# An encoder trunk on one NeuronCore: what each stage loads for the next one, and who waits for the last stores

## What is computed

```python
for i in range(2):
    h = rmsnorm(x, ln_g[i])
    p = h @ (w_in_a if i == 0 else w_in_b)      # mixer inputs, q_mem (256), gate (1024)
    o_mix = mla_mixer(...) if i == 0 else sgu_mixer(...)          # both 768 wide
    o_mem = memory_attention(q_mem, mem, mem_norm_g[i], w_mem_kv[i], ...)   # 4 heads of 64
    o = concatenate([o_mix, o_mem], -1) * silu(gate)
    x = x + o @ w_out[i]
# sgu_mixer: u, v = gelu(uv); v = rmsnorm(v);
#   out = u * (w_s[g] @ v[chunk of 128 tokens, group g] + b_s)
```

## Time and profile before

| | |
|---|---|
| median of 3 runs | 3411.08 us (3408.62 to 3411.88) |
| the profiled execution | 3414.65 us, of which the span is 3412.9 us |
| TensorE busy (matmul / weight load) | 3222.1 us, 94% / 2763.4 us |
| VectorE, ScalarE, GpSimd busy | 1990.6, 1713.4, 1407.5 us |
| mean granted clock | 0.967 of full speed |
| mean DMA rate | 133 GB/s |

### The profile page before, as it was taken

How to read it: one execution, slowest core, us unless ns; L and a number is a source line. 1 busy time by engine, 2 the same in 40 slices (tenths; PEclk the granted TensorE clock), 3 DMA queues, 4 the chain that set the end, 5 groups by cost and what they waited for, 6 DMA issues and landing times. The chain is left out here.

```text
span 3412.9 us, 46378 instructions
## 1 busy us (share of the span) xinstructions
PE 3222.1 (94%) x17548; PEld 2763.4 (81%) x17548; DVE 1990.6 (58%) x2792; ACT 1713.4 (50%) x2472; POOL 1407.5 (41%) x916
## 2 busy tenths in 40 slices
PE   7979979999999999999899997997999979999899
PEld 7978857777777777777589996786888859999787
DVE  5638868888888888888553333444333334333432
ACT  4526647777777777777654443003232234544200
POOL 2238858999999999999710000000111000000000
PEclk9989979999999999999899998998999989999899
DMA  8958972323232233331142224886222243222565
GB/s 298 340 197 317 346 263 59 69 65 70 64 59 52 49 66 69 66 69 26 59 186 92 106 90 144 229 228 212 95 95 97 85 148 139 91 93 81 172 191 155
DMA packets 380334, 454.87 MB, mean 133 GB/s; under 512 B 51800, under 2 KB 317400, under 8 KB 367824
## 3 DMA queue, kind: packets, MB, share of 16 engines
q1 hardware_dynamic: 380112, 451.91, 42.8%
HBM read 262.07 MB, written 189.64 MB: 132 GB/s over the span
## 5 line engine op out<-in xcount | busy, mean ns | idle before, releaser
L1331 POOL TENSOR_TENSOR at_acc<-at_acc,at_ph 128x1024 f32<-128x1024 f32 x288 | 691.4, 2401 | 64.4 <-ACT at_ph L1255 48.9
L1376 DVE TENSOR_TENSOR at_pl<-at_sc,at_ph 128x1024 fp32r<-128x1024 f32 x408 | 499.0, 1223 | 127.0 <-ACT at_sc L1256 122.7
L1255 ACT ACTIVATE at_ph<-at_sc 128x1024 fp32r<-128x1024 f32 x408 | 418.5, 1026 | 291.9 <-PE at_sc L1175 283.4
L1364 DVE TENSOR_REDUCE at_mx<-at_mxp 128x1 f32<-128x512 f32 x816 | 521.6, 680 | 36.3 <-PE at_mxp L1186 36.1
L1256 ACT ACTIVATE at_sc<-at_sc 128x1024 f32<-128x1024 f32 x408 | 416.0, 1020 | 0.0
L171 PE MATMUL gm_gate<-gm_h,gm_g_hi 128*128 128x256 f32 x1280 | 367.9, 287 | 6.4 <-DVE gm_g_lo L160 6.4
L172 PE MATMUL gm_gate<-gm_h,gm_g_hi 128*128 128x256 f32 x1280 | 362.2, 283 | 0.0
L173 PE MATMUL gm_gate<-gm_h,gm_g_lo 128*128 128x256 f32 x1280 | 362.1, 283 | 0.0
L1200 PE MATMUL at_o_hi<-at_ph,at_v 128*128 128x512 f32 x816 | 323.4, 396 | 0.1
L1202 PE MATMUL at_o_lo<-at_pl,at_v 128*97 128x512 f32 x816 | 322.4, 395 | 0.0
L1692 POOL TENSOR_TENSOR gm_rstd<-gm_mean,all_mhalf 128x4 f32<-128x4 f32 x40 | 40.3, 1007 | 619.1 <-DVE gm_mean L1832 619.1
(11 more groups left out here) (248 smaller groups left out, 7781.4 us busy)
## 6 DMA issues: line engine op xcount, KB each, us to landing
gm_h<-hT SPq DMA_DIRECT2D x48, 1024.0 KB, 7.2
hT<-lat_n_h SPq DMA_DIRECT2D x28, 1024.0 KB, 7.2
qT<-hd_stq SPq DMA_DIRECT2D x60, 384.0 KB, 6.5
kT<-hd_stk SPq DMA_DIRECT2D x60, 384.0 KB, 5.7
ka_q<-qT SPq DMA_DIRECT2D x120, 192.0 KB, 3.0
sgT<-gm_sg SPq DMA_DIRECT2D x80, 256.0 KB, 2.1
ou_o<-omix SPq DMA_DIRECT2D x40, 512.0 KB, 6.4
ou_sg<-sgT SPq DMA_DIRECT2D x40, 512.0 KB, 7.2
```

What stands on the lines that cost most here:

```text
L1255: act.activation(ph[:, g], sc[g % 2][:], ACT.Exp, scale=SCALE).then_inc(p_hi, 1)
L1331: pool.tensor_tensor(acc[:, c.slot, :], f32(ph[:, (g - 1) % 4]).rearrange("p b n -> p (b n)") if t == 1 else acc[:, c.slot, :], now, ALU.a ...
L1364: dve.tensor_reduce(mx[:, c.slot, n:n + 1], mxp[n % 2][:], AX.X, ALU.max).then_inc(mx_in, 1)
L1376: dve.tensor_tensor(pl[:, g], sc[g % 2][:], f32(ph[:, g]), ALU.subtract).then_inc(p_lo, 1)
```

## The change

- In `attention` SP loads the four memory tiles of gm0, one in part 2 of each of the first four heads, into two buffers that now live across stages (`flow.first`, `flow.second`, one tile pair each; gm's `h` blocks use them too).
- In gm, at the head of the last block, SP loads o and sg of ou's tiles 0 and 1 into `flow.first`, and in layer 0 the reciprocal sums of tile 0 into `flow.share`. ou keeps using these buffers for all its tiles.
- In ou0 SP loads the first two row tiles of x1 and the gains after tile 6; ScalarE squares them after tiles 10 and 11, VectorE scales them after 12 and 13, TensorE turns the first within its last tile, and it is split there. These steps are gone from the start of sg.
- At the end of sg SP loads the first two memory tiles of gm1, behind its last stores; the other two stay at the start of gm1.
- The waits for a stage's last stores move into the next stage, ahead of the first load that could read them. The last stage keeps its own.
- ou0's `gated` multiplies r by the gate, then o by that, in three instructions where there were two.
- sg's gelu takes four instructions, cut at the PSUM banks, and TensorE begins a tile bank by bank: for the first two of eight k steps it does all of bank 0, then 1, then 2, each after the gelu that frees it. The last half of the last mixing goes into `acc` banks 0 and 1 instead of `mix`.
- `NormTranspose` of sg has a Space of its own (ns), and `Flow` has one too, so there is one more clearing of semaphores with its meeting of engines behind sg, and one more at the end of the program.

```diff
@@ attention, SP
+                    if c.part == 2 and c.head < MEM_TILES:
+                        flow.load_memory(sp, c.head, mem_rows)
...
-                for u in range(2):
-                    n = 48 * (Chunk.COUNT) // 2 - (16 if u == 0 else 0)
-                    sp.wait_ge(o_out[u], n + (16 if u != last.slot else 0))
@@ gate_memory, SP        (AHEAD = MEM_TILES if layer == 0 else 2)
-                for i in range(MEM_TILES):
-                    sp.dma_start(f32(h[:, i // 2, i % 2]), hT[first_row + i]).then_inc(m_in[i], 16)
+                for i in range(AHEAD, MEM_TILES):
+                    flow.load_memory(sp, i, mem_rows)
...
                 w.load_rest(sp)
+                if layer == 0:
+                    flow.wait_mixed(sp)
+                else:
+                    flow.wait_spatial(sp)
...
                 def step(b):
+                    if b == NB - 1:
+                        sp.wait_ge(gate_mm, b * PAIRS)
+                        for u in range(2):
+                            sp.wait_ge(o_out[u], 16)
+                            sp.wait_ge(sg_out[u], 16 * PAIRS // 2)
+                        if inv_s is not None:
+                            sp.wait_ge(inv_out, 16)
+                        for i in range(2):
+                            flow.load_gates(sp, layer, i, omix, sgT)
+                        if inv_s is not None:
+                            flow.load_share(sp, 0, inv_s, flow.share)
...
-                for u in range(2):
-                    sp.wait_ge(o_out[u], 16 * NB)
-                    sp.wait_ge(sg_out[u], 16 * NB * PAIRS // 2)
@@ gated_output, SP
-                load_o(0)
-                load_o(1)
+                if inv_s is not None:
+                    flow.load_share(sp, 1, inv_s, r[1])
                 w.load_rest(sp)
...
                 w.load_following(sp)
+                flow.wait_gates(sp, layer)
...
+                    if ahead and i == 6:
+                        for n in range(2):
+                            sp.wait_ge(y_out[n], 16)
+                        ahead.load(sp, 0)
+                        ahead.load_gains(sp, 0)
+                        ahead.load(sp, 1)
@@ gated_output, TensorE
                     for k in range(KD):
+                        if ahead and i == TILES - 1 and k in (1, 5):
+                            ahead.turn(pe, 0, k // 5)
@@ gated_output, VectorE
-                        dve.tensor_tensor(o[:, u, 0:DIV], o[:, u, 0:DIV], r[:, u], ALU.mult
-                                          ).then_inc(divided, 1)
+                        dve.tensor_tensor(r[u][:], r[u][:], sg[:, 0:DIV], ALU.mult).then_inc(divided, 1)
...
+                        dve.tensor_tensor(out[:, 0:DIV], o[:, 0:DIV], r[u][:], ALU.mult)
+                    dve.tensor_tensor(out[:, split:], o[:, split:], sg[:, split:], ALU.mult).then_inc(mixed, 1)
@@ spatial, SP
-                norm.all_stored(sp)
                 for u in range(2):
-                    sp.wait_ge(out[u], 16 * TILES // 2)
+                    sp.wait_ge(mm, TILES - 1 + u)
+                    sp.wait_ge(norm.stored[u], 16 * TILES // 2)
+                    flow.load_memory(sp, u, mem_rows)
@@ spatial
+        FREE = (1, 3, 4)
@@ spatial, TensorE
-                        after(pe, o_in, pair * SGG + half * GR)
+                        if at_end(pair, half):
+                            pe.wait_ge(gelu, 4 * TILES)
+                        else:
+                            after(pe, o_in, pair * SGG + half * GR)
...
-                        after(pe, gelu, 2 * i)
-                        for k in range(KD):
+                        if i == 0:
+                            w.ready(pe, "uv", 1)
+                        for c in range(3):
+                            after(pe, gelu, 4 * (i - 1) + FREE[c])
+                            for k in range(2):
+                                columns(i, k, c)
+                        for k in range(2, KD):
@@ spatial, ScalarE
-                    act.activation(uo[:, i % 4, :], flat[:, 0:MIX], ACT.Gelu_apprx_tanh).then_inc(gelu, 1)
+                    act.activation(uo[:, i % 4, 0:BLK], acc[:, 0, :], ACT.Gelu_apprx_tanh).then_inc(gelu, 1)
+                    act.activation(uo[:, i % 4, BLK:], acc[:, 1, 0:MIX - BLK], ACT.Gelu_apprx_tanh
+                                   ).then_inc(gelu, 1)
```

More of the change, by code:

```diff
@@ L2024, in _, with spatial @@
                         low(i + 1)
+                    if ahead and i == TILES - 1:
+                        for half in range(2):
+                            ahead.take_lo(dve, 0, half)
                     add(i)
[L2028 removed]
+                    if ahead and i in (12, 13):
+                        if i == 12:
+                            dve.wait_ge(ahead.gains_in[0], 16)
+                        ahead.scale(dve, i - 12)
+def spatial(nc, K, A, plan, following, norm, flow, mem_rows, omix):
     G2, GR = SGG // 2, SGG // 2
```

200 lines of the change are left out of this document (123 added, 77 removed).

## The result

The changed kernel takes 3350.39 us (median of 4 runs, 3349.18 to 3355.4), the kernel before 3410.66 (4 runs, 3408.62 to 3411.88): a ratio of 0.9825, with an interval of 0.9813 to 0.9837. The profiled execution took 3355.4 us with a span of 3353.6, against 3412.9 before.

What follows compares the result with a forecast made beforehand. TensorE, busy 94% of the span, was taken as the bound. The terms summed to 48.4 us, taking the profiled 3414.65 to 3366.3; with the median 3.6 lower, the forecast was 3362.7 us, range 3356 to 3372.

Steps and rivals of the forecast that it cites:

- Inside sg: In sg, TensorE's eleven waits on gelu go, as the first bank is free earlier: gain 6.7 us (5 to 7).
- The price of leaving a stage: At each handover, time from last issue to next stage's start without waiting for a landing: 1.3 us (1.0 to 1.7).
- Attention to gm0: Start of gm0: earlier first product and no wait for the first turn of keys, gain 5.9 us (4 to 7).
- gm0 to ou0: Start of ou0: TensorE begins earlier after gm0's last issue, gain 10.7 us (10 to 11.5).
- ou0 to sg: Start of sg: earlier first product, and the wait at tile 1's turn gone, gain 12.4 us (10.5 to 14).
- sg to gm1: Start of gm1: earlier first product, memory rows landing 4.9 us after issue, gain 5.3 us (3.5 to 7).
- The wait of 4.3 stays: In gm1, the 4.3 us wait behind the gate weights stays, since the same 4 MB stand ahead of them.
- The end: End of the program: one more clearing of semaphores costs 0.5 us.
- (a): Rival, chance 0.12: in ou0, early loads delay tile 9's loads, stalling 1.3 up to 4 us; 3364 to 3367.
- (b): Rival, chance 0.08: a stage can't be left with stores under way, so some 9 us come back; 3372.
- (c): Rival, chance 0.05: early loads do not set the starts; half the five handovers' gain, or 20 us, lost; 3383.
- (d): Rival, chance 0.02: denser TensorE work in sg is granted half clock speed, making the kernel 7 us slower, 3418.

Runs made afterwards that it cites:

- b_gelu: The kernel before with only gelu cut at the banks and tiles begun bank by bank, no buffer moved: 3401.58 us against 3412.19.
- b_h32: The kernel before with 32 unused bytes per partition ahead of sg's row buffer: 3403.38 us against 3411.04.
- b_gelu_h32: The kernel before with gelu by banks and 32 bytes of padding ahead of sg's row buffer, no handover changed: 3397.32 us against 3410.18.
- a_h0: The changed kernel with 32 unused bytes per partition ahead of `h_first` and 32 behind it: 3353.79 us.
- a_both: The changed kernel with next-stage weight loads behind tiles 2 and 3's loads in ou0, and memory tiles loaded before sg's last two stores: 3339.68 us.
- a_wait: The changed kernel with attention, both gate stages, ou0 and sg again waiting for their last stores before they end: 3359.51 us against 3412.19.

## Why the prediction was wrong, step by step

**The step that failed** is "Inside sg", "The eleven waits go: 6.7 (5 to 7)". It measured 17.4, and with the turn at tile 1 that stands in the handover's term, 18.4 between first and last product. Two things make it up:

- *The size of the pauses.* The mechanism was right, the first bank is free before TensorE comes back. Its price was read from the list of waits, which counts from modelled ends; from start to start it is 9.8 (b_gelu). The term was short by 3.1. I gave the reported 6.7 us nearly as its upper bound, and that was the fault: the timeline of before had both kinds of turn, and four transposes of 0.11 us each are no reason for a product to start 1.21 or 0.54 us behind the first of them.
- *The step of the matmuls.* The change took the rows into a buffer shared across stages, and by chance of allocation they now begin a multiple of 256 bytes from the weights. That is luck, not a part of the plan: 6 ns less for each of 1440 products, 7.4 us alone (b_h32), 8.9 on top of gelu by banks (b_gelu to b_gelu_h32, and a_h0 to after). No term of mine, no rival and no bound had room for it. It could be seen before: ou stepped at 227 and sg at 234 in the same profile, on matmuls of the same shape. The earlier trace rows even stood beside the question, 99 matmuls in 22 us.

9.8 and 8.9 make the 18.7 us of b_gelu_h32; the changed kernel's stage gained 18.4. So nothing else is needed to account for it. The term was 10.7 us short, which is nearly all of the 12.3 by which the forecast missed; the other terms together make 0.2, and 1.4 come from the profiled execution, which lies 5.0 above the median and not 3.6 as before. Only the 3.1 of the pauses have to do with the mechanism that I forecast.

**What held.** "The price of leaving a stage", 1.3 with 1.0 and 1.7 as bounds: 1.1 behind gm0, 0.9 behind ou0, 1.7 behind gm1, and with two Spaces 1.6 behind attention (1.7 forecast) and 1.9 behind sg (1.8). "Attention to gm0", "gm0 to ou0", "ou0 to sg" and "gm1 to ou1" came within 0.4 us each. TensorE started 4.1 after the last issue in gm0 (4.0 forecast), 7.0 in ou0 (7.4), 6.5 in ou1 (6.2), and in sg 6.3 after the last addition's end (6.6).

**What was off by a little.** "sg to gm1": the memory rows land 5.9 us after the first of their issues, where 4.9 was taken, so the start gained 4.4; the text named that as its weak point. "The wait of 4.3 stays" was half wrong: it fell to 2.3. Two of the four megabytes are issued before the stage's end now; a_both, which issues them earlier still, has no such wait at all. "The end": 1.1 for the extra clearings, for 0.5.

**The rivals.** (a) A backlog in ou0 came, and was hidden. In the changed kernel VectorE waited at tile 9:

```profile
2193.62 0.96 DVE L2074 TENSOR_TENSOR ou_r<-ou_r,h_first 128x768 f32<-128x768 f32 x1 [4.74 <-DMA ou_r<-inv_s]
```

That is 4.3 more than the 0.47 of the earlier trace rows, under the 4.4 us of cover that the rival worked out, and TensorE's products for tiles 9 and 10 came within 0.1 us of their old distance. The mechanism was right and the cover just held. The low part of the tile is written until 2198.25, and its first product starts at 2198.34:

```profile
2197.02 1.23 DVE L2084 TENSOR_TENSOR ou_og<-ou_full,ou_og 128x1024 fp32r<-128x1024 f32 x1 [1.11 <-ACT ou_og L2045]
...
2198.34 0.47 PE L171 MATMUL ou_acc<-ou_o_hi,ou_og 128*128 128x512 f32 x1
```

A tenth of a microsecond more and a stall would have shown. (b) is refuted by a_wait, and by the changed kernel itself: ou0 starts 1.1 us after an issue that takes 2.2 to land. (c) did not come: in every handover the start moved. (d) did not come: the granted clock in sg is 1.00 in the stretch between 2420 and 2700 us of both kernels, with no pause left.

**The range** left out the upside: its 0.03 for "more than I find" was the case that came.

## What to carry to other kernels

A wait in the list of waits is idle time behind a modelled end. Where a short matmul or transpose stands before it, read the pause from start to start and compare it with a turn that does not wait; pauses of a few tenths of a microsecond that repeat per tile may be worth half as much again as listed, and some are not listed. When a change moves or shares buffers, compare the start-to-start step of equal matmuls across the stages of the same profile, and look at the distance of the two operands modulo 256 bytes: in sg a pad of 32 bytes was worth 2 to 3% of the stage's products, and an unrelated allocation can take it away again. Measure it per stage: attention gained less, and the gate products, with 256 moving columns, are 1.4 ns slower where the two lie alike. A load that is moved ahead has its price at the transfer now standing behind it: a_both took away 5.3 us of a stall of 9.2, and the rest came up again two tiles later.

## What the runs showed of the hardware

- Matmuls of 128 rows, 128 columns and 512 moving columns in the split-value format step at 227 ns in sg when both operands begin alike modulo 256 bytes in a partition, and at 233 to 234 otherwise (tried: 64, 128 and 224 modulo 256), at a granted clock of 1.00 in all. In the records a matmul's own duration moves with it, as in sg before and after:

```profile
L172 PE MATMUL sg_acc<-sg_uv_lo,sg_n_h 128*128 128x512 f32 x480 | 190.2, 396 | 0.0
```

```profile
L172 PE MATMUL sg_acc<-sg_uv_lo,h_first 128*128 128x512 f32 x480 | 187.5, 391 | 0.0
```

- All row tiles of sg lie alike modulo 256, so its kernels do not tell whether the distance counts to the row tile in use or to the next one.
- With 256 moving columns (the gate products) it is the other way about: 118.4 ns at 224 modulo 256, 119.8 at 0 (a_h0).
- In attention the same placing gave 1 to 5 ns, and nothing for score products. That other traffic or the number of rows is behind it is a guess that no run here tested.
- A stage was left, its semaphores cleared and the next one begun 0.9 to 1.9 us after the last DMA issue; at gm0's end that is 2.1 us earlier than with the wait for the store (1.1 for 3.2). The semaphores of those stores belong here to a Space that lives on.
- Stages whose code is identical still moved from run to run: sg's first product came between 2349 and 2361 us in kernels that do not differ ahead of it. Single times of this kernel tell little below 5 us; the stretch inside a stage repeats within 0.5 (400.0 to 400.5 us in the four kernels with slow steps and the old gelu).
